# Row maxima of a forgetting-attention stage: short rows first, head 0 inside the query units

## The chip, the cores and the metric

One core of one Trainium2 chip runs the whole program; each of its engines (TensorE, VectorE, ScalarE, GpSimd, and SyncE, which issues most DMAs) has its own instruction queue. The metric is device time of one execution in microseconds; the times before are a median of three.

## The reference

A two-layer decoder trunk for one prompt of 1,040 rows (16 learned ones ahead of 1,024) and 8 decode sequences of 4 rows; width 1,024, 16 heads of 64. Layer 0 is a short gated convolution with an MLP, layer 1 forgetting attention with an MLP. Between them keys, values and the logarithms of forget values are computed. For the change only the prompt's attention counts:

```python
def forget_attention(q, k, v, c_q, c_k, q_pos, k_pos):
    s = jnp.einsum('nqhd,nkhd->nhqk', q, k) * (HEAD_DIM ** -0.5)
    s = s + (c_q.T - c_k.T)            # c = cumsum of log forget values, per head
    causal = k_pos[None, :] <= q_pos[:, None]
    s = jnp.where(causal[None, None], s, NEG_INF)
    p = jax.nn.softmax(s, axis=-1)
    return jnp.einsum('nhqk,nkhd->nqhd', p.astype(v.dtype), v)
```

## The kernel before

Every float32 matrix is split into a rounded high part (fp32r) and the difference, the low part; a product is hi*hi + hi*lo + lo*hi. A *unit* is 128 output columns of a projection: `load_unit` (SP) fetches 512 KB of weights, `round_unit` (ScalarE) makes the high part, `cut_unit` (VectorE) the low part, `unit` (TensorE) runs 72 accumulating products of 358 columns into three banks, slots alternate, and `mid` places small jobs at chosen eighths of it.

**Query units** (`U_Q` to `U_Q+7`, two heads each). Behind unit n, VectorE scales the result (`scaled`), ScalarE squares it twice (`head_squares`), VectorE takes the low part (`head_lo`), TensorE sums over each head's 64 rows (`head_sums`, at eighths 6 and 7 of the next unit, banks 6 and 7), ScalarE takes the root (`head_root`), VectorE multiplies (`head_fin`). `stage_hi` and `stage_lo` split the queries into two pairs of staging buffers, and `stage_out` writes them to DRAM (`qh_rows`, `ql_rows`), from where the heads are loaded. These pairs share their place with head 1's operands.

**Attention.** Logits are computed transposed, keys on partitions, in eight pieces per head (`GROUPS`); the softmax needs the row maximum first. So for each head `max_logits` computes the high-part logits with queries on partitions, in uses (`USES`) of one bank each, `reduce_max` (VectorE) takes their maxima, shift products (`"A"`, `"B"`, `"C"` in `USES`) turn the maxima into a row on TensorE, and `keep_shift` (ScalarE) copies that row into the query operand, negative, so that every logit comes out with the maximum taken off. The 1,040 query rows are tiled from 0 in eight tiles of 128 and one of 16. The tile of 16 rows needs three passes over all keys, 512, 512 and 16 columns. `RING = 2`: a use may start when the use two before it, in the same of banks 4 and 5, has been reduced or copied.

What sets the order is written out by hand. TensorE at turn t: logits of piece t+2, value products of piece t (`weigh_values`, three passes for each key tile), then the uses of the next head that `USE_AT[g]` names. ScalarE at turn t: two exponentials (`exp_logits`), at g = 3, 5, 7 of the piece before a `keep_shift`. VectorE at turn t: `probs_lo(t+1)`, the reductions of `USE_AT[g]`, at g = 3 the values' low part, at g = 4 `invert_sums` of the former head, at g = 7 `divide` for it.

SP per head h (`attention_loads`, L913 on): the sums of head h-1 spread to 65 partitions, its inverse stored and loaded again (`load_inverse`, L957 and L960, it waits for `invert_sums`), and only then `load_head(h + 2)` (L931 to L933, four DMAs, behind the logits of head h; the first maxima of head h+2 wait for all four, `h_loaded`), the values of a pair of heads, and `load_cross`.

```python
                if h:
                    spread_sums(h - 1)
                    load_inverse(h - 1)
                if h + 2 < HEADS:
                    load_head(h + 2)
```

Head 0 has no head before it. After the last query unit TensorE waits for three constants that ScalarE rounds there (L1657 to L1659), then runs all 18 uses of head 0 one behind the other with the last unit's head sums between them, while VectorE and ScalarE also finish and stage the last two query blocks.

## Time and profile before

| | |
|---|---|
| median of three runs | 2926.96 us (2926.76 to 2930.78) |
| the profiled execution | 2932.93 us |
| its span | 2931.1 us |
| TensorE busy | 2783.4 us (95%) |
| VectorE busy | 1186.8 us (40%) |
| ScalarE busy | 786.3 us (27%) |
| granted TensorE clock, mean | 0.979 of full |

The page is of one execution. Busy times are sums over the span; the attention of the prompt lies from 1536 to 1887 us, decode attention behind it to 2057, projections and MLPs before and after. A line of the timeline is one instruction, with the idle time of its engine before it and what ended that. A granted clock of 1.00 is 2.4 GHz, 0.50 is 1.2 GHz.

### The profile page before, as it was taken

The page shows a single profiled execution, that of the slowest core. Times are in us where ns is not written, and L with a number is a line of the kernel's source. Part 1 is how long each engine was busy: PE and PEld are TensorE (multiplying, and loading weights), DVE is VectorE, ACT ScalarE, POOL GpSimd, SP SyncE. Part 2 cuts the span into 40 slices and gives each one's busy share as a digit, 9 for nine tenths or more (in the row PEclk, how much of TensorE's full clock was granted, in tenths as well). Part 3 has the DMA queues.
Part 4 walks back from the last instruction along what each step waited for, and adds up shares of the span by engine and source line. Part 5 has one row for each costly group of instructions (what it writes and reads, how often), then busy time and mean ns, then how long its engine had stood idle before and what let it go on. Part 6 is the DMA issues. An engine that isn't in the chain of part 4 may idle for free.

```text
span 2931.1 us, 41586 instructions
## 1 busy us (share of the span) xinstructions
PE 2783.4 (95%) x17026; PEld 2701.3 (92%) x17026; DVE 1186.8 (40%) x1340; ACT 786.3 (27%) x1127; POOL 98.2 (3%) x68
## 2 busy tenths in 40 slices
PE   6999999999999999999998899767999999999999
PEld 5999999999999999998996888645999999999998
DVE  4444435224133243343346777543343133242331
ACT  4111121111011112362355566543321011110111
POOL 3000020000000001100000000000110000000000
PEclk9999999999999999999998999888999999999999
DMA  3111111111111111143244454332111111111112
GB/s 98 45 47 46 43 44 43 43 43 49 45 43 43 43 46 48 44 156 113 62 147 115 122 119 96 88 119 72 36 38 49 43 43 43 43 50 43 44 43 74
DMA packets 256005, 188.52 MB, mean 64 GB/s; under 512 B 15088, under 2 KB 237232, under 8 KB 255906
## 3 DMA queue, kind: packets, MB, share of 16 engines
q1 hardware_dynamic: 236802, 178.14, 21.5%
q10 hardware_dynamic: 19104, 8.99, 1.1%
q8 instruction: 71, 1.16, 0.2%
q14 instruction: 28, 0.23, 0.0%
HBM read 156.47 MB, written 30.49 MB: 64 GB/s over the span
## 4 chain that ended last, share of the span: by engine, by line
PE 88%; DVE 3%; DMA 3%; ACT 2%; issue 1%; POOL 1%; SPq 1%; ACTq 0%; DVEq 0%; POOLq 0%
PE ps L416 77%; DMA q_hi_ext<-k_hi_ext 2%; PE ps L878 1%; PE ps L801 1%; PE ps L579 1%; DVE max_parts L597 1%; POOL t L451 1%; PE ps L638 1%; PE ps L715 1%; PE ps L716 1%; PE ps L717 1%; PE ps L470 1%; PE ps L639 1%; DVE probs_lo L678 1%; PE ps L502 0%
## 5 line engine op out<-in xcount | busy, mean ns | idle before, releaser
L401 DVE TENSOR_TENSOR w_lo<-w_raw,w_hi 128x1024 fp32r<-128x1024 f32 x192 | 235.1, 1225 | 1233.4 <-ACT w_hi L393 1233.4
L416 PE MATMUL ps<-x_hi,w_hi 128*128 128x358 f32 x2688 | 593.8, 329 | 18.5 <-DVE x_lo L444 18.4
L416 PE MATMUL ps<-x_hi,w_lo 128*128 128x358 f32 x2688 | 590.3, 328 | 0.0
L416 PE MATMUL ps<-x_lo,w_hi 128*128 128x358 f32 x2688 | 589.5, 328 | 0.0
L393 ACT ACTIVATE w_hi<-w_raw 128x1024 fp32r<-128x1024 f32 x192 | 203.4, 1060 | 1325.2 <-PE ps L416 1324.4
L416 PEld LDWEIGHTS ps<-x_hi,w_hi 128*128 128x128 f32 x2688 | 465.4, 191 | 22.1 <-DVE x_lo L444 11.8
L416 PEld LDWEIGHTS ps<-x_lo,w_hi 128*128 128x128 f32 x2688 | 466.6, 190 | 0.0
L416 PEld LDWEIGHTS ps<-x_hi,w_lo 128*128 128x128 f32 x2688 | 465.9, 190 | 0.0
L416 PE MATMUL ps<-hid_hi,w_hi 128*128 128x358 f32 x1920 | 423.4, 329 | 3.1 <-DVE hid_lo L1234 3.1
L416 PE MATMUL ps<-hid_hi,w_lo 128*128 128x358 f32 x1920 | 420.8, 327 | 0.0
L416 PE MATMUL ps<-hid_lo,w_hi 128*128 128x358 f32 x1920 | 420.2, 327 | 0.0
L416 PEld LDWEIGHTS ps<-hid_hi,w_hi 128*128 128x128 f32 x1920 | 332.5, 190 | 3.3 <-issue 3.3
L416 PEld LDWEIGHTS ps<-hid_hi,w_lo 128*128 128x128 f32 x1920 | 332.7, 190 | 0.0
L416 PEld LDWEIGHTS ps<-hid_lo,w_hi 128*128 128x128 f32 x1920 | 332.0, 190 | 0.0
L1475 ACT ACTIVATE hid_hi<-t 128x1074 f32 (+1 forms) x72 | 79.4, 1103 | 291.1 <-DVE t L1783 260.2
L1697 DVE TENSOR_TENSOR hid_lo<-t,hid_hi 128x1074 f32 (+1 forms) x72 | 92.0, 1278 | 100.1 <-ACT hid_hi L1475 100.1
L579 PE MATMUL ps<-k_hi_ext,q_hi_ext 128*128 128x512 f32 (+5 forms) x240 | 89.5, 397 | 41.4 <-DVE max_parts L597 12.8
L451 POOL TENSOR_TENSOR t<-t,t 128x1074 f32<-128x1074 f32 x25 | 70.3, 2811 | 1275.8 <-ACT t L435 1275.4
L597 DVE TENSOR_REDUCE max_parts<-ps 128x1 f32<-128x512 f32 (+5 forms) x176 | 96.2, 563 | 39.0 <-PE ps L582 21.1
L1757 DVE TENSOR_TENSOR acc<-ps,acc 128x1074 f32 (+1 forms) x80 | 101.6, 1270 | 22.4 <-PE ps L416 22.4
L678 DVE TENSOR_TENSOR probs_lo<-probs_f,probs_hi 128x768 fp32r<-128x768 f32 (+3 forms) x128 | 97.7, 764 | 23.8 <-ACT probs_hi L666 15.6
L579 PEld LDWEIGHTS ps<-k_hi_ext,q_hi_ext 128*128 128x128 f32 (+1 forms) x240 | 41.8, 178 | 62.0 <-DVE max_parts L597 23.6
(228 smaller groups left out, 2461.9 us busy)
## 6 DMA issues: line engine op xcount, KB each, us to landing
w_raw<-in_mlp_w SPq DMA_DIRECT2D x128, 512.0 KB, 3.8
w_raw<-in_conv_w_in SPq DMA_DIRECT2D x24, 512.0 KB, 3.6
w_raw<-in_w_kv SPq DMA_DIRECT2D x16, 512.0 KB, 4.7
k_page<-in_cache_k SPq DMA_DIRECT2D x16, 512.0 KB, 4.2
v_page<-in_cache_v SPq DMA_DIRECT2D x16, 512.0 KB, 4.2
kh_rows<-staged_hi SPq DMA_DIRECT2D x8, 520.0 KB, 2.6
kl_rows<-staged_lo SPq DMA_DIRECT2D x8, 520.0 KB, 3.1
qh_rows<-staged_hi SPq DMA_DIRECT2D x8, 520.0 KB, 2.6
```

The lines of the kernel that those rows point to most:

```text
L393: act.activation(WH[:, s], RAW[:, s], ACT.Copy).then_inc(w_hi, 1)
L401: dve.tensor_tensor(WL[:, s], RAW[:, s], WH[:, s].bitcast(F32), ALU.subtract).then_inc(w_lo, 1)
L416: mm = pe.matmul(PS[:, G * s + g, 0:GW], w[:, s, k], x[:, k, g * GW:(g + 1) * GW], start=(k == 0 and n == 0), stop=(k == KC - 1 and n == 2))
L451: pool.tensor_tensor(T2[:, 0:T], T2[:, 0:T], squares(f, m), ALU.add).then_inc(x_ssq, 1)
L470: mm = pe.matmul(PS[:, b, 0:GW], weights[:, :], x[:, g * GW:(g + 1) * GW], start=not stop, stop=stop)
L579: mm = pe.matmul(PS[0:rows, bank, 0:b - a], QA[hh][:, P * i:P * i + rows], CK[hh][:, a:b], start=True, stop=not diagonal)
L597: dve.tensor_reduce(to, PS[0:rows, bank, 0:b - a], mybir.AxisListType.X, ALU.max).then_inc(red_done, 1)
L638: mm = pe.matmul(PS[0:keys, b, col:col + n], CK[hh][:, k], QA[hh][:, q0:q0 + n], start=True, stop=False)
L678: dve.tensor_tensor(PBL[:, t % HI_RING, 0:nb * w], PF[:, t % 2, 0:nb * w], PBH[:, t % HI_RING, 0:nb * w].bitcast(F32), ALU.subtract).then_ ...
L1475: act.activation(HH[:, j], T1[:, :], ACT.Copy).then_inc(hid_hi, 1)
L1697: dve.tensor_tensor(HL[:, j], T1[:, :], HH[:, j].bitcast(F32), ALU.subtract).then_inc(hid_lo, 1)
L1757: dve.tensor_tensor(banks(ACC[:, m]), result(c), banks(ACC[:, m]), ALU.add).then_inc(unit_read, 1)
```

## The change

1. **Tiling of the maxima.** Rows 0 to 15 are the short tile, tiles 1 to 8 have 128 rows from row 16 on (`max_rows`). Keys 0 to 15 of all rows go into one bank, use `"M"`: nine products of 16 columns and one of the mask, two reductions. The other uses begin at key 16. 18 uses become 16; part A now covers rows 0 to 399, B to 783, C the rest. Each part has one joining reduction (`JOIN_AT`).
2. **Place of the uses.** `weigh_values` runs a use behind each key tile's three passes, no longer all behind the last.
3. **Head 0.** Its uses go into query units 4 to 7 (`FIRST_USES`), in banks 6 and 7, their reductions and shifts into VectorE's and ScalarE's query turns; the head sums there wait for them. Behind the last unit come part C, the logits of pieces 0 and 1, then the head sums.
4. **Order of the hand-over.** ScalarE does the exponentials of pieces 0 and 1 ahead of the last root; finishing, staging and one weight split of VectorE go behind the first value pieces.
5. **Staging.** The last two query blocks use a third pair of buffers (`staged_in`), in the places of `INV` and `OS`; head 0's loads go on SP behind the fifth weight load, head 1's before the last two stagings; SP waits for both before head 2's loads.
6. **Constants.** The identity is one fp32r tile; the sign moves into `keep_shift` (scale -1); the mask takes the place of `ones` during attention and `ones` is set again behind it.

```diff
-USES = [(i, 0, P * (i + 1)) for i in range(4)]
-USES += [(i, a, b) for i in (4, 5) for a, b in ((0, 512), (512, P * (i + 1)))] + ["A"]
-USES += [(i, a, b) for i in (6, 7) for a, b in ((0, 512), (512, P * (i + 1)))]
-USES += [(8, 0, 512), "B", (8, 512, SEQ), (8, SEQ, NPR), "C"]
+USES = ["M", (1, 0, 128), (2, 0, 256), (3, 0, 384), (4, 0, 512), (5, 0, 512), (5, 512, 640), (6, 0, 512), "A",
+        (6, 512, 768), (7, 0, 512), "B", (7, 512, 896), (8, 0, 512), (8, 512, SEQ), "C"]
...
+JOIN_AT = {3: "A", 9: "B", 14: "C"}
+USE_AT = [(0, 1), (2, 3), (4, 5), (6, 7, 8), (9, 10), (11, 12), (13, 14), (15,)]
+FIRST_USES = [(), (), (), (0, 1, 2, 3), (4, 5, 6, 7), (8, 9, 10, 11), (12, 13, 14), (15,)]
...
+            elif x == "M":
+                for i in range(1, NT):
+                    q, rows = max_rows(i)
+                    pe.matmul(PS[:, bank, TAIL * (i - 1):TAIL * i], QA[hh][:, q:q + rows], CK[hh][:, 0:TAIL],
+                              start=True, stop=True)
+                to = PS[0:TAIL, bank, P:P + TAIL]
+                pe.matmul(to, QA[hh][:, 0:TAIL], CK[hh][:, 0:TAIL], start=True, stop=False)
+                mm = pe.matmul(to, IDR[:, 0:TAIL], MASK[:, 0:TAIL], start=False, stop=True)
...
-            mm.then_inc(pv_done, 1)
+                done = j == GROUPS[g][-1][1]
+                if done:
+                    mm.then_inc(pv_done, 1)
+                k = j - GROUPS[g][0][1]
+                for u in uses[k:] if done else uses[k:k + 1]:
+                    max_logits(h + 1, u)
...
+        def staged_in(n):
+
+            return 2 if n >= 2 * KC - 2 else n % 2
...
+            probs_lo(0)
             dve.wait_ge(vo_ones, 4)
             values_lo(0)
-            probs_lo(0)
             for t in range(NG * HEADS):
                 h, g = divmod(t, NG)
                 if t + 1 < NG * HEADS:
                     probs_lo(t + 1)
+                if t == 0:
+                    head_fin(2 * KC - 1, 1, G_QN, QS[:, KC - 1])
+                    stage_lo(2 * KC - 2, QS[:, KC - 2, 0:NPR])
...
+                if t == 1:
+                    cut_unit(U_O + 1)
+                    stage_lo(2 * KC - 1, QS[:, KC - 1, 0:NPR])
...
+            first_max(KC - 1)
+            pe.wait_ge(unit_read, U_O - 1)
+            logits(0)
             pe.wait_ge(unit_read, U_O)
-            for u in range(NUSE):
-                max_logits(0, u)
-                if u == 4:
-                    for f in norm_sums.values():
-                        f()
-            logits(0)
             logits(1)
+            pe.wait_ge(nm_kept, N_SH)
+            for f in norm_sums.values():
+                f()
```

TensorE's queue, head 0's first value pieces with head 1's first maxima (`probs` products are the value pieces, `k_hi_ext`/`q_hi_ext` products into `ps` the maxima). Before:

```order
L717 MATMUL ps<-probs_lo,v_hi 128x384
L715 MATMUL ps<-probs_hi,v_hi 128x256
L716 MATMUL ps<-probs_hi,v_lo 128x256
L717 MATMUL ps<-probs_lo,v_hi 128x256
L715 MATMUL ps<-probs_hi,v_hi 128x128
L716 MATMUL ps<-probs_hi,v_lo 128x128
L717 MATMUL ps<-probs_lo,v_hi 128x128
L579 MATMUL ps<-k_hi_ext_57,q_hi_ext_56 128x128
L582 MATMUL ps<-mask,ident_r 128x128
L579 MATMUL ps<-k_hi_ext_57,q_hi_ext_56 128x256
L582 MATMUL ps<-mask,ident_r 128x128
```

The same place in the changed kernel:

```order
L731 MATMUL ps<-probs_lo,v_hi 128x384
L587 MATMUL ps<-k_hi_ext_57,q_hi_ext_56 128x16 x8
L590 MATMUL ps<-k_hi_ext_57,q_hi_ext_56 16x16
L591 MATMUL ps<-mask,ident 16x16
L729 MATMUL ps<-probs_hi,v_hi 128x256
L730 MATMUL ps<-probs_hi,v_lo 128x256
L731 MATMUL ps<-probs_lo,v_hi 128x256
L596 MATMUL ps<-k_hi_ext_57,q_hi_ext_56 128x128
L599 MATMUL ps<-mask,ident 128x128
L729 MATMUL ps<-probs_hi,v_hi 128x128
L730 MATMUL ps<-probs_hi,v_lo 128x128
L731 MATMUL ps<-probs_lo,v_hi 128x128
```

The head's first maximum, which waits for the loads, moved from behind the third value tile to behind the first, and is now eight products of 16 columns with 128 rows loaded for each.

ScalarE's queue from the last query turn on (`squares`, `t_r`: the two squares; `t<-ps,eps` and `t<-t`: the root; `probs`: exponentials). Before:

```order
L1561 ACTIVATE squares_90<-k_work 128x1074 [waits z_fin,unit_read]
L1563 ACTIVATE t_r<-k_work 128x1074 [waits z_fin]
L1657 ACTIVATE mask<-mask_f_149 128x128 [waits p_const]
L1658 ACTIVATE ident_r<-ident 128x128
L1659 ACTIVATE minus_ident<-ident 128x128
L1569 ACTIVATE staged_hi_61<-q_all 128x1040 [waits st_kept0,z_fin]
L393 ACTIVATE w_hi<-w_raw 128x1024 [waits unit_done,w_loaded1]
L1575 ACTIVATE t_83<-ps,eps 128x358 [waits aux_done] x3
L1578 ACTIVATE t_83<-t_83 128x1074 [waits aux_read]
L1569 ACTIVATE staged_hi_63<-q_all 128x1040 [waits st_kept1,z_fin]
```

In the changed kernel:

```order
L1581 ACTIVATE squares_91<-k_work 128x1074 [waits z_fin,unit_read]
L1583 ACTIVATE t_r<-k_work 128x1074 [waits z_fin]
L675 ACTIVATE probs_f_115<-ps 128x768 [waits st_done]
L680 ACTIVATE probs_hi<-ps 128x768
L704 ACTIVATE v_hi<-v_raw 128x9x64 [waits v_loaded]
L675 ACTIVATE probs_f_115<-ps 128x768 [waits st_done]
L680 ACTIVATE probs_hi<-ps 128x768
L1595 ACTIVATE t_84<-ps,eps 128x358 [waits aux_done] x3
L1598 ACTIVATE t_84<-t_84 128x1074 [waits aux_read]
L1589 ACTIVATE staged_hi_123<-q_all 128x1040 [waits z_fin]
L403 ACTIVATE w_hi<-w_raw 128x1024 [waits unit_done,w_loaded1]
L1589 ACTIVATE staged_hi_123<-q_all 128x1040 [waits st_kept0,z_fin]
```

Two pairs of exponentials and the first values now stand before the root; two stagings and a weight rounding stand behind it, ahead of the exponentials of piece 2.

VectorE's queue in the changed kernel behind the last head's low part (`k_work` squares), where the maxima of head 0 stood before:

```order
L711 TENSOR_TENSOR v_lo<-v_raw,v_hi 128x9x64
L692 TENSOR_TENSOR probs_lo<-probs_f_115,probs_hi 128x768
L1859 SCALAR_TENSOR_TENSOR q_all<-k_work,vectors,t_84 128x1074
L1866 TENSOR_TENSOR staged_lo_124<-q_all,staged_hi_123 128x1040
L610 TENSOR_REDUCE max_parts<-ps 128x8
L612 TENSOR_REDUCE row_max<-ps 16x1
L617 TENSOR_REDUCE max_parts<-ps 128x1
L692 TENSOR_TENSOR probs_lo<-probs_f_115,probs_hi 128x768
L617 TENSOR_REDUCE max_parts<-ps 128x1 x2
L622 TENSOR_REDUCE row_max<-max_parts 128x3
L411 TENSOR_TENSOR w_lo<-w_raw,w_hi 128x1024
L1866 TENSOR_TENSOR staged_lo_124<-q_all,staged_hi_123 128x1040
```

Its last finishing, two stagings and a weight split stand between the first differences of probabilities.

## Rows read from the trace of the kernel before

**Rows 1.** The page, chain that ended last: shares by line.

```profile
PE ps L416 77%; DMA q_hi_ext<-k_hi_ext 2%; PE ps L878 1%; PE ps L801 1%; PE ps L579 1%; DVE max_parts L597 1%; POOL t L451 1%; PE ps L638 1%; PE ps L715 1%; PE ps L716 1%; PE ps L717 1%; PE ps L470 1%; PE ps L639 1%; DVE probs_lo L678 1%; PE ps L502 0%
```

**Rows 2.** Table by stretch: length, busy us by engine, granted clock, DMA share, GB/s.

```profile
1510.30:1523.20 12.90, 12.90 (x81) 12.90 (x79) 6.09 (x5) 6.84 (x9) 0.00 (x0) 1.00 0.55 158
...
1540.00:1550.00 10.00, 6.65 (x20) 5.15 (x20) 6.91 (x12) 4.58 (x9) 4.20 (x5) 0.50 0.47 161
```

**Rows 3.** Chain in order of time: start us, us, what; the last query unit's last stretch.

```profile
1534.70 1.50 PE ps L416 x9
```

**Rows 4.** Timeline of PE, start of attention: start us, us, instruction, [idle before].

```profile
1540.53 0.48 PE L579 MATMUL ps<-k_hi_ext,q_hi_ext 128*128 128x128 f32 x1 [4.34 <-ACT minus_ident L1659]
...
1565.33 0.41 PE L715 MATMUL ps<-probs_hi,v_hi 128*128 128x384 f32 x1
...
1573.16 0.28 PE L715 MATMUL ps<-probs_hi,v_hi 128*128 128x256 f32 x1
```

**Rows 5.** Groups by line, 1250 to 1950 us: busy us, mean ns, idle before.

```profile
L661 ACT ACTIVATE probs_f<-ps 128x768 f32<-128x768 f32 (+3 forms) x128 | 84.8, 663 | 37.8 <-PE ps L639 19.1 <-PE ps L642 18.1
...
L1575 ACT ACTIVATE t<-ps,eps 128x358 f32<-128x358 f32 x42 | 22.1, 558 | 53.4 <-PE ps L470 53.4
...
L1563 ACT ACTIVATE t_r<-k_work 128x1074 fp32r<-128x1074 f32 x13 | 14.3, 1102 | 1.7
...
L1825 DVE TENSOR_TENSOR squares_r<-squares,t_r 128x1074 fp32r<-128x1074 f32 x7 | 9.0, 1279 | 8.7 <-ACT t_r L1563 8.7
```

**Rows 6.** Timeline of PE, one head's period, 1671 to 1693 us.

```profile
1671.24 0.29 PE L715 MATMUL ps<-probs_hi,v_hi 128*128 128x256 f32 x1
...
1672.42 0.33 PE L579 MATMUL ps<-k_hi_ext,q_hi_ext 128*128 128x128 f32 x1 [0.37 <-DMA q_hi_ext<-k_hi_ext]
...
1679.70 0.40 PE L573 MATMUL ps<-minus_ident,row_max 128*1 128x128 f32 x4
...
1680.78 0.45 PE L579 MATMUL ps<-k_hi_ext,q_hi_ext 128*128 128x384 f32 x1 [0.39 <-ACT q_hi_ext L618]
...
1685.99 0.40 PE L579 MATMUL ps<-k_hi_ext,q_hi_ext 128*16 128x512 f32 x1 [0.79 <-DVE max_parts L597]
...
1692.89 0.33 PE L579 MATMUL ps<-k_hi_ext,q_hi_ext 128*128 128x128 f32 x1 [0.72 <-DMA q_hi_ext<-k_hi_ext]
```

**Rows 7.** Timeline of SP's queue in that period: the store, the last head load.

```profile
1684.77 0.36 SPq L957 DMA_DIRECT2D inv_rows<-inv_spread  x1
...
1688.38 0.56 SPq L933 DMA_DIRECT2D q_hi_ext<-k_hi_ext  x1
```

**Rows 8.** Timelines of ACT and of DVE in that period, behind part A.

```profile
1680.14 0.58 ACT L618 ACTIVATE q_hi_ext<-ps 1x512 fp32r<-1x512 f32 x1 [2.35 <-PE ps L573]
...
1682.46 0.72 DVE L678 TENSOR_TENSOR probs_lo<-probs_f,probs_hi 128x544 fp32r<-128x544 f32 x1
```

**Rows 9.** Timeline of PE: products of 16 columns, two forms.

```profile
1668.00 0.17 PE L579 MATMUL ps<-k_hi_ext,q_hi_ext 128*16 128x16 f32 x1
1668.03 0.17 PE L582 MATMUL ps<-mask,ident_r 128*16 128x16 f32 x1
...
1669.58 0.26 PE L716 MATMUL ps<-tail_hi,v_lo 128*128 128x16 f32 x1
1669.69 0.26 PE L717 MATMUL ps<-tail_lo,v_hi 128*128 128x16 f32 x1
```

**Rows 10.** Timeline of PE: first maxima of three other heads.

```profile
1607.35 0.33 PE L579 MATMUL ps<-k_hi_ext,q_hi_ext 128*128 128x128 f32 x1 [1.44 <-DMA q_hi_ext<-k_hi_ext]
...
1834.21 0.33 PE L579 MATMUL ps<-k_hi_ext,q_hi_ext 128*128 128x128 f32 x1 [1.01 <-DMA q_hi_ext<-k_hi_ext]
...
1855.54 0.33 PE L579 MATMUL ps<-k_hi_ext,q_hi_ext 128*128 128x128 f32 x1 [1.54 <-DMA q_hi_ext<-k_hi_ext]
```

**Rows 11.** Table by stretch, one us (columns as in rows 2).

```profile
1609.00:1610.00 1.00, 1.00 (x7) 1.00 (x6) 1.00 (x2) 0.00 (x0) 0.00 (x0) 0.50 0.50 74
```

**Rows 12.** Timeline of SP's queue: the store in the head of 1607.

```profile
1621.25 0.35 SPq L957 DMA_DIRECT2D inv_rows<-inv_spread  x1
```

More of the change, by code:

```diff
@@ L175, in trunk @@
         WL, _ = place("w_lo", [P, 2, KC, P], F32R)
-        ident, _ = place("ident", [P, P])
+        IDR, _ = place("ident", [P, P], F32R)
+        ident = IDR[:, :].bitcast(F32)
+        ones0 = at[0]
         ones, _ = place("ones", [P, P], F32R)
+        MASK, _ = place("mask", [P, P], F32R, offset=ones0)
         heads1, _ = place("ones_per_head", [P, P], F32R)
@@ L540, in head, with bank_of, reds_through @@
             return h // 2, h % 2
-        def use_of(h, u):
-            x = USES[u]
-            n_sh = sum(isinstance(y, str) for y in USES[:u + 1])
-            return x, 4 + u % RING, (N_RED * h + u + 1 - n_sh, N_SH * h + n_sh)
+        def bank_of(h, u):
+            return (4 if h else 6) + u % RING
+        def reds_through(h, u):
+            return N_RED * h + sum(REDS[:u + 1])
         def ring_wait(h, u):
@@ L1089, in attention_scalar @@
         def attention_scalar():
-            keep_shift(0, "A")
-            values_hi(0)
-            keep_shift(0, "B")
-            keep_shift(0, "C")
-            for t in range(NG * HEADS):
+            for t in range(2, NG * HEADS):
                 exp_logits(t)
@@ L1915, in _ @@
                 head_lo(U_Q, KC + n, n % 2)
-                if n:
+                if n == KC - 1:
+                    for hh in range(2):
+                        _, other = halves(hh)
+                        dve.memset(VH[:, hh, NT - 1, other].bitcast(F32), 0.0).then_inc(v_zero, 1)
+                    dve.memset(P8H[:, :, :].bitcast(F32), 0.0).then_inc(v_zero, 1)
+                    dve.memset(P8L[:, :, :].bitcast(F32), 0.0).then_inc(v_zero, 1)
+                    dve.wait_ge(v_zero, 5)
+                    for hh in range(2):
+                        _, other = halves(hh)
+                        dve.memset(VH[0:LASTP, hh, NT - 1, other].bitcast(F32), 1.0).then_inc(v_zero, 1)
+                elif n:
+                    for u in FIRST_USES[n][0:2]:
+                        reduce_max(0, u)
                     stage_lo(KC + n - 1, QS[:, n - 1, 0:NPR])
+                    for u in FIRST_USES[n][2:]:
+                        reduce_max(0, u)
                     cut_unit(U_Q + n + 2)
@@ L2058, in _, with first, norm @@
             unit(U_Q + 1, mid=head_sums(U_Q, 0, ax(AX_Q, 0, 0), KC))
-            with pe.Fori(1, KC // 2) as i:
-                unit(U_Q, i, mid=head_sums(U_Q, 1, ax(AX_Q - 3, 6, i), KC + 2 * i - 1))
-                unit(U_Q + 1, i, mid=head_sums(U_Q, 0, ax(AX_Q, 6, i), KC + 2 * i))
+            for n in range(1, KC - 1):
+                sums, mid = head_sums(U_Q, n % 2, ax(AX_Q + 3 * n, 0, 0), KC + n), {}
+                for k in range(len(FIRST_USES[n])):
+                    def first(n=n, k=k):
+                        first_max(n, k)
+                    mid[2 + k] = first
+                def norm(n=n, f=sums[6]):
+                    if FIRST_USES[n]:
+                        pe.wait_ge(red_done, reds_through(0, FIRST_USES[n][-1]))
+                        pe.wait_ge(nm_kept, sum(USES[u] in SHIFTS for u in range(FIRST_USES[n][-1] + 1)))
+                    f()
+                unit(U_Q + n + 1, mid={**mid, 6: norm, 7: sums[7]})
             attention_tensor(head_sums(U_Q, 1, ax(AX_Q + 3 * (KC - 1), 0, 0), 2 * KC - 1))
```

305 lines of the change are left out of this document (154 added, 151 removed).

## The prediction

> **What bounds the kernel now.** I read the page first: its chain of waits lies 77% on the projection products, and the one entry that is not arithmetic is a DMA at 2%, the last of the four loads of a head [rows 1]. The table by stage shows where TensorE is not full: during the query projection a unit of 12.9 us is full while VectorE works 6.1 us of it, so there is room for more; from 1540 us TensorE works 6.65 us of 10 at a granted clock of 0.50 [rows 2]. The chain in order of time gives the end of the last query unit, 1534.70 + 1.50 = 1536.20 us [rows 3]. The timeline of TensorE then shows the gap: the first maxima 4.34 us later, the first value product at 1565.33, that of the fourth piece of head 0 at 1573.16 [rows 4]. So two things can be won: this gap, 29.1 us for 13 maxima of head 0 and their turns on three engines; and the waits in heads 1 to 15.
>
> For a head in full swing I read the timeline of one period [rows 6] beside SP's queue [rows 7]. Its maxima begin when the loads land, at 1672.42. 12.35 us later, at 1684.77, SP can store the inverse of the former head's sums, and only behind that it issues the next head's loads; they land at 1692.89, 8.1 us after the store. The next maxima wait for them, here 0.72 us. From 1607.35 to 1855.54 [rows 10] twelve periods take 248.2 us, 20.7 each. So this is a ring of two parts: **load to store** (TensorE, ScalarE, VectorE) and **store to load** (DMA). A second ring is TensorE alone: 20.5 us in this period without the 0.72 is 19.75, in which it also idles 0.39 for ScalarE and 0.79 for VectorE [rows 6], and in shorter waits.
>
> **The change part by part.**
>
> *Head 0's maxima in units 4 to 7.* 4,608 columns; two value pieces in the timeline that are three passes of 256 and three of 128 columns take from 1671.24 to 1672.05 [rows 6], about 0.12 us per 256 columns, so 2.2 us; 8 mask products at 0.11 (0.9), 7 shift products at 0.06 (0.4). The first-16-keys bank: eight products that load 128 fresh rows each for 16 streamed columns. The tail's products have just this form and start 0.11 us apart [rows 9]: 0.9, with two small ones 0.95. Sum **+4.4 us** at full clock, on the path since TensorE is full there. VectorE's reductions, some 1.5 to 2 us a unit, are hidden by the 6.8 us it is idle in a unit [rows 2]. Head 0's eight loads are moved on SP to before three weight loads; a weight load behind them may land some 2 us later than its rounding wants it, which costs nothing while the unit before it runs. The head sums of these units now also wait for the last reduction, since both use the same two banks; it ends about 1 us before they are due.
>
> *From the last unit to the fourth piece.* Now ScalarE's and VectorE's turns decide. A full pass takes 1.10 us on ScalarE, 1.28 on VectorE, an exponential 0.66 to 0.8, a root piece 0.56 [rows 5]. From the unit's end: scaling, to 1.6; two squares, to 3.9; the low part, to 5.3; head sums on TensorE, to 6.4. ScalarE meanwhile does two pairs of exponentials and the first values, to 7.8, then the roots, to 9.5; the value products may start. Logits of piece 2 come first, at half clock after that idle: value products at 10.9 (before: 29.1). Then ScalarE has root pass, staging, a weight rounding, staging, to 13.8, exponentials of piece 2 to 15.4; VectorE follows with the difference (1.0), two reductions (1.0), a weight difference and a staging (2.5): 19.8, then 0.5 for piece 3. The fourth piece's value products start at 20.3 instead of 37.0: **-16.7 us**. The staging that went behind is the price inside this term: without it they would start near 17. SP now waits for the last staging too before it loads head 2; that is stored some 24 us after the unit's end, and head 0's last logits, for which these loads wait anyway, come no sooner.
>
> *One head's period.* Load to store: 7.3 us from the first maximum to the shift products of part A before [rows 6]. The change adds the 16-key bank (0.95) and the second and third value pieces, which now stand behind it (0.7 to 0.8), takes away 256 columns and a mask (0.2) and about 0.3 net of short waits: 8.3. From A to the store it was 5.1: the copy of the shifts starts 0.44 after A and takes 0.58, then two exponentials, and VectorE begins the next difference (0.72) at 1682.46 [rows 8], behind a values difference, then two reductions of 512. Now VectorE stands ready when ScalarE ends, and one reduction is of 256 columns: 4.4. Sum 12.7 against 12.35. Part two, 8.1 us, is untouched: the loads still stand behind the store on SP. Ring: 20.8. TensorE's own ring gets shorter: two passes of 512 and the lone 16 columns go (-0.55), the bank comes (+0.95), the waits of 0.79 and 0.39 and the shorter ones go (-1.7), some 0.3 of new ring waits come: 19.75 becomes about 18.7. So **TensorE will stand still some 2 us at each head's first maximum**, where it now stands 0.2 to 0.7 in most: the time won in the head is returned to the DMA. Behind the waiting product stand the other two value pieces and the next piece's logits, so nothing fills the wait; the exponentials, two pieces ahead, run dry too.
>
> *What that wait does to the clock.* In the present trace waits of 1.44 and 1.54 us in this place [rows 10] are each followed by half clock (0.50 at 1609 [rows 11], the lower of the two levels, 1.2 GHz), after 1.01 it stays full. The store after the 1.44 us wait came at 1621.25 [rows 12], 13.9 us after the first maximum instead of 12.35: 1.5 us lost. I take that for every head: 12.7 + 1.5 + 8.1 = 22.3 us against 20.7, times twelve, **+19 us**. Lower end of this term 0 (no drop: 20.8), upper +27 (the store-to-load part 8.8 as in the head of 1607).
>
> For the price of the eight small products a rule speaks against mine. The Trainium skill, "TensorE: Matmul & The Clock Gate", section on the back-to-back issue gap, gives matmuls of 1 to 64 columns about 60 cycles, 25 ns at the full clock; by it alone the bank would take 0.25 us and the sum would be about 9 us lower. The rows show 0.11 where 128 rows are loaded anew and 0.03 where 16 are [rows 9], so the rule alone does not hold for this form.
>
> *Rest.* Between the fourth piece and head 2's first maximum, short waits gone and the maximum placed earlier: -1.5. After the last first maximum: -0.3. Restoring the ones: +0.1.
>
> **Sum:** 4.4 - 16.7 + 19 - 1.5 - 0.3 + 0.1 = **+5**. The profiled execution took 2932.9 us (span 2931.1), 6.0 above the median of the three runs, 2926.96; the difference is applied to the median: 2932.
>
> **The rivals.**
>
> *A, forecast (55%)*: as above. Its own range is 2922 to 2940: 0.4 us either way in load to store and 0.4 in the clock's cost are some 9 us over twelve heads. Of it 8 points are faster, 27 same, 20 slower.
>
> *B, the clock holds (27%)*: the wait at the first maximum is under about 1.2 us in most heads, because load to store is 0.8 shorter than I make it or the drop needs more than idle time. For it: only three drops are seen, all beside a 0.75 us idle some 7 us earlier, which the change removes. Against it: every wait of 1.4 or more dropped, and right behind the wait now comes the bank of tiny products. Time: without the 19, 2913 to 2916. Faster.
>
> *C, the small products cost 0.03 each (6%)*: the weight loads hide. Bank 0.3 instead of 0.95, twelve times: 2924. It decides if the loads of the eight hide behind their products; the first of the four tail rows says they do once in a while. By the rule quoted above from the Trainium skill it would come out so.
>
> *D, slower (7%)*: one mechanism, SP's chain. In the head of 1607 the loads landed 8.8 us after the store, not 8.1. If the loads, now asked for by a TensorE that does nothing else, land like that in all heads, the period is 23.0 and the time 2941. It decides from 8.3 us on.
>
> *E, the change does not do what it says at the start (5%)*: the maxima are ready but piece 0 still waits on ScalarE, whose roots stand behind exponentials that wait for the values' load. Half of the 16.7 is lost: 2940.
>
> **How the numbers follow.** About 0.2%, 6 us, is what a measurement of this kernel can tell from no change. Faster 0.08 + 0.25 (B) + 0.02 (C) = 0.35; same 0.27 + 0.02 + 0.04 = 0.33; slower 0.20 + 0.07 + 0.05 = 0.32. The predicted time is A's. The range takes in B and most of D and E: 2908 to 2943.
>
> **What would show it.** First maximum's wait in each head: A 1.7 to 2.5 us and 0.50 clock behind it, B under 1.2 and full clock. Bank of eight: 0.95 us. First maximum to store: 12.7 at full clock, 14.2 with a drop. First value product 10.9 us after the last query unit, fourth piece at 20.3. Query units with maxima about 1.1 us longer each, no idle in them. If the waits of 0.79 and 0.39 are still there, the period's working is wrong; if the store-to-load part is shorter than 7.5 us, the whole term is.

## The result, and the profile after

The changed kernel takes **2952.5 us** (median of 4 runs, 2948.8 to 2958.8) beside 2928.9 us of the kernel before on the same chip: ratio 1.0083, 95% interval 1.0063 to 1.0103. It is slower by 24 us. The forecast was 2932 with a range up to 2943. The profiled execution took 2952.93 us, its span 2951.1 at a mean granted clock of 0.967; before it was 2931.1 at 0.979. The difference of the two spans, 20.0 us, is what the points below account for.

The chain that ended last, here by engine, from the page of the changed kernel, does not show where the time went; it follows another branch than in [rows 1], its shares add up to about a third of the span, and the DMA is at 0%:

```profile
PE 33%; ACT 1%; DVE 1%; issue 1%; DMA 0%; POOL 0%; ACTq 0%; DVEq 0%; POOLq 0%; SPq 0%
```

The waits of TensorE between 1595 and 1850 us do show it (waited for, us in total, times, longest); first the kernel before:

```profile
PE ps L579 <- DVE max_parts L597: 10.5, 13, 1.1
PE ps L579 <- DMA q_hi_ext<-k_hi_ext: 7.4, 11, 1.6
PE ps L579 <- ACT q_hi_ext L618: 4.6, 12, 0.4
PE ps L579 <- DVE row_max L597: 1.6, 10, 0.2
```

and the same view of the changed kernel, its one entry of any size:

```profile
PE ps L587 <- DMA q_hi_ext<-k_hi_ext: 18.8, 12, 2.5
```

TensorE now waits less in sum (18.8 us for 24.1), but in one piece per head. The granted clock in the table by stretch over the same 255 us (columns as in [rows 2]), before:

```profile
1595.00:1850.00 255.00, 229.21 (x1636) 210.45 (x1636) 194.36 (x360) 153.14 (x311) 0.00 (x0) 0.99 0.49 112
```

and now:

```profile
1595.00:1850.00 255.00, 236.16 (x1548) 221.71 (x1546) 168.31 (x325) 140.33 (x281) 0.00 (x0) 0.87 0.47 107
```

So TensorE is busier (236 us for 229) and gets less done (1548 entries for 1636): behind its waits it runs at the lower level. Counted by single microseconds, half clock (0.50, 1.2 GHz) fills 10 us between 1595 and 1870 before, 68 us now, in all twelve heads, eight times for 6.8 us and four times for 3.4. One head's period in the timeline of TensorE, against [rows 6, 10]:

```profile
1668.42 1.06 PE L587 MATMUL ps<-k_hi_ext,q_hi_ext 128*128 128x16 f32 x8 [1.35 <-DMA q_hi_ext<-k_hi_ext]
1669.33 0.17 PE L590 MATMUL ps<-k_hi_ext,q_hi_ext 128*16 128x16 f32 x1
...
1679.65 0.37 PE L582 MATMUL ps<-ident,row_max 128*1 128x16 f32 x4
...
1691.67 1.06 PE L587 MATMUL ps<-k_hi_ext,q_hi_ext 128*128 128x16 f32 x8 [1.57 <-DMA q_hi_ext<-k_hi_ext]
```

and SP's queue in it, against [rows 7]: the store of the inverse, and the last of the four loads that the first maximum waits for.

```profile
1683.84 0.35 SPq L987 DMA_DIRECT2D inv_rows<-inv_spread  x1
...
1687.94 0.56 SPq L963 DMA_DIRECT2D q_hi_ext<-k_hi_ext  x1
```

First maximum to part A 11.2 us (before 7.3), to the store 15.4 (12.35), store to the next first maximum 7.8 (8.1): a period of 23.25 here. Over twelve heads the mean is (1872.32 - 1598.40) / 12 = 22.8 us; before it was 20.7.

The start, from the timeline of TensorE, against [rows 3, 4]: the end of the last query unit, the first value product, that of the fourth piece.

```profile
1540.38 0.65 PE L426 MATMUL ps<-x_hi,w_lo 128*128 128x358 f32 x3
...
1553.85 0.63 PE L729 MATMUL ps<-probs_hi,v_hi 128*128 128x384 f32 x1
...
1566.24 0.39 PE L729 MATMUL ps<-probs_hi,v_hi 128*128 128x256 f32 x1
```

### The profile page after: what moved, and what is told of

Same layout as the page of the kernel before. It is cut to its first block and busy times, and to the rows that moved or that the text cites. A ratio compares the mean times of both kernels' runs of the same rounds, so it can differ in the third digit from the quotient of the medians.

```text
span 2951.1 us, 41757 instructions
## 1 busy us (share of the span) xinstructions
PE 2815.4 (95%) x17122; PEld 2741.9 (93%) x17122; DVE 1175.4 (40%) x1342; ACT 786.5 (27%) x1125; POOL 99.3 (3%) x68
## 5 line engine op out<-in xcount | busy, mean ns | idle before, releaser
L426 PEld LDWEIGHTS ps<-x_hi,w_hi 128*128 128x128 f32 x2688 | 464.6, 190 | 22.4 <-DVE x_lo L454 11.8
L617 DVE TENSOR_REDUCE max_parts<-ps 128x1 f32<-128x512 f32 (+1 forms) x192 | 105.8, 554 | 63.6 <-PE ps L599 54.6
L729 PE MATMUL ps<-probs_hi,v_hi 128*128 128x272 f32 (+4 forms) x272 | 100.9, 371 | 1.7 <-DVE probs_lo L692 1.5
L652 PE MATMUL ps<-q_hi_ext,k_hi_ext 128*128 128x272 f32 (+5 forms) x288 | 97.9, 345 | 0.8 <-ACT t L1595 0.7
```

Of the source, the lines that this page charges most:

```text
L426: mm = pe.matmul(PS[:, G * s + g, 0:GW], w[:, s, k], x[:, k, g * GW:(g + 1) * GW], start=(k == 0 and n == 0), stop=(k == KC - 1 and n == 2))
L617: dve.tensor_reduce(NMX[:, i - 1, k:k + 1], PS[:, bank, 0:b - a], axis, ALU.max).then_inc(red_done, 1)
L652: mm = pe.matmul(PS[0:keys, b, col:col + n], CK[hh][:, k], QA[hh][:, q0:q0 + n], start=True, stop=False)
L729: pe.matmul(to, VH[:, hh, j], ph, start=(j == 0), stop=False)
```

## The experiments

All times are medians, the ratios are to the kernel before on the same chip; its own median lay between 2928.9 and 2934.1 us in the different series, so a distance of two medians from different series carries up to 5 us of that, which the ratios do not. "Period" is the mean distance of the first maxima of neighbouring heads in the profiled execution. "Half clock" is counted by single microseconds, over the stretch named.

**1. The loads of the next head but one ahead of the inverse sums (in SP's queue), in the changed kernel.**

```
     if h: spread_sums(h - 1)
-    if h: load_inverse(h - 1)
     if h + 2 < HEADS: load_head(h + 2)
+    if h: load_inverse(h - 1)
```

> The changed kernel with one step moved in SP's queue: the loads of head h+2's keys and queries are issued before the load of the inverse sums of head h-1, behind which they stand now (they then wait only for the logits of head h that read the same buffers). Ring theory: the 1.1 to 2.5 us wait at each head's first maximum is the store-to-load ring (7.8 us from the store to the landing); with the loads ahead of it the wait is under 0.3 us in most heads, the clock stays at its upper level, the period falls from 22.8 to 18.7 to 20 us, and the time to 2905 to 2920. Rival 'the placement itself is slow' (the uses between the value pieces, or the small products, stretch the head): the wait goes but the period stays over 22 us, time within 8 us of the changed kernel. Rival 'the transfers are bound by the DMA': the loads land no earlier, the wait stays.

2927.6 us, ratio 0.9990 (0.9977 to 1.0002): 25 us under the changed kernel. The profiled execution took 2917.8 us, the fastest of ten (up to 2935.8). In it no wait for the loads is left and the period is 20.3 us. The theory holds for the ring, but the period and the median are above the expected ranges, since a new wait came, for VectorE's difference (TensorE's waits in this run):

```profile
PE ps L729 <- DVE probs_lo L692: 17.8, 13, 2.2
```

The waits of VectorE name what holds that difference back: the division stands ahead of it in VectorE's order, and the inverse sums, whose load now lies behind the head's loads, come late.

```profile
DVE q_all L760 <- DMA inv_sums<-inv_rows: 40.7, 13, 4.0
```

**2. Products that fill the wait.** Seven 128x512 products whose results nothing reads, ahead of the wait for the loads. They write into the bank of the first maxima, so the wait for that bank, `ring_wait(h, u)`, which stood last, moves ahead of them; the kernel computes nothing else differently.

```
+    ring_wait(h, u)
     if u == 0:
+        if h > 2:
+            for _ in range(7): pe.matmul(PS[:, bank, 0:512], VH[:, 1 - hh, 0], CK[1 - hh][:, 0:512], ...)
         pe.wait_ge(h_loaded[hh], 64 * (h // 2 + 1))
-    ring_wait(h, u)
```

> The changed kernel with seven products of 128x512 more in every head from the fourth on, whose results nothing reads, placed before the wait for the loads at the first maximum; they take about 1.5 us of TensorE at full clock. The wait itself is untouched, so this tells the clock's part from the wait's. If the idle at the first maximum is what drops the granted clock, the 7 us of half clock behind it go, load to store falls from about 15.3 to about 12.7 us, and the period from 22.8 to about 20.8: time 2925 to 2935 although TensorE does more. If the drop comes from something else (the bank of eight products with 16 columns, or the thin work of the whole head), the half clock stays and the time is that of the changed kernel or up to 10 us more.

2924.9 us, ratio 0.9973 (0.9962 to 0.9983). TensorE does some 1.5 us more in each of 13 heads and the kernel is 28 us faster than the changed one. The loads land no sooner after the store (8.2 us in the mean for 8.0), but the clock holds in nine of the twelve heads from 1595 us on:

```profile
1595.00:1850.00 255.00, 250.68 (x1768) 231.31 (x1767) 182.06 (x354) 150.87 (x305) 0.00 (x0) 0.97 0.50 114
```

In the heads without a drop first maximum to part A is 8.1 us and to the store of the inverse 12.0 to 12.3 (in one 8.5 and 12.7); the period is 20.0 to 20.3 in six of the nine, and up to 21.9 in the other three, whose next loads land later. That is the changed kernel's ring at full clock, and it is shorter than the 20.7 us of the kernel before. The loss against that kernel is therefore the clock's.

**3. The maxima behind the value piece again**, everything else as changed.

```
-                k = j - GROUPS[g][0][1]
-                for u in uses[k:] if done else uses[k:k + 1]:
-                    max_logits(h + 1, u)
+            for u in uses:
+                max_logits(h + 1, u)
```

> The changed kernel, but every head's maxima of a turn stand behind the whole value piece again, not between its parts, as in the kernel before; order of the maxima, first-keys bank and head 0 stay changed. If the wait at the first maximum rules, the maxima come 0.7 to 0.8 us later into the head and the loads wait is the same or shorter: time within 5 us of the changed kernel. If placing them between the value pieces is itself the loss, the time falls by 10 us or more. If it was a gain hidden in the sum, it rises by about 5 to 10 us, the short waits of 0.4 and 0.8 us for ScalarE and VectorE coming back.

2935.1 us, ratio 1.0016 (1.0002 to 1.0030): 17 us faster than the changed kernel, which the theory did not expect. The value products now stand ahead of the waiting product and fill part of the wait, so waits are 0.65 to 1.45 us in most heads where they were 1.1 to 1.6:

```profile
PE ps L587 <- DMA q_hi_ext<-k_hi_ext: 14.6, 12, 2.5
PE ps L582 <- DVE max_parts L617: 3.4, 12, 0.3
```

Half clock between 1595 and 1870 falls from 68 to 44 us, and first maximum to part A at full clock is 7.75 instead of 8.1. 24 us less half clock are 12 us of time, twelve times 0.35 are 4: most of the 17. The forecast had named that nothing fills the wait behind the first maximum and priced that at nothing.

**4. The same move of the loads in the kernel before.**

> The kernel before with the same one step moved in SP's queue as in the first of these runs. Ring theory: here the ring is nearly balanced by TensorE's own 19.75 us, so moving the loads takes away waits of 0.2 to 0.7 us in most heads, 1.4 in two, and the three drops of the clock: period from 20.7 to about 19.8, time 2914 to 2920. Against the changed kernel with the same step this gives what the change is worth without the ring: by the theory the changed one is then 5 to 12 us faster. If the rival holds that the change itself stretches the head, the changed kernel with this step stays slower than this one.

2965.6 us, ratio 1.0115 (1.0098 to 1.0132): 34 us slower than the kernel before, a miss. Its period is 23.2 us:

```profile
PE ps L579 <- DVE row_max L597: 27.7, 11, 3.0
PE ps L579 <- DVE max_parts L597: 8.5, 11, 0.8
```

The theory took the landing of the loads for the only thing on SP's queue that matters. VectorE waits 2.6 us in the mean for the inverse sums in the division; the differences and the reductions of the row maxima stand behind it.

**5, 6. Both moves: loads ahead, and the division one turn later on VectorE**, in the changed kernel and in the kernel before.

```
-    if h and g == 7:
-        divide(h - 1)
+    if h > 1 and g == 0:
+        divide(h - 2)
```

> The changed kernel with the loads of head h+2 ahead of the inverse sums in SP's queue, and now also the division of head h-1, which waits for those sums, one turn later on VectorE, behind the next difference instead of ahead of it. With the loads alone moved, the division waited 3.2 us and held back the difference behind it, and TensorE stood 1.1 to 1.7 us for that difference in every head. Ring theory: this wait goes too, waits of TensorE over 0.5 us vanish from most heads, half clock between 1595 and 1870 us falls from 20 us to under 7, the period from 20.2 to 18.8 to 19.3 us, time 2905 to 2915. Rival 'VectorE itself is full there': the difference comes late again behind the division, one turn further, the period stays over 20 us and the time within 5 us of the run with the loads alone moved (2928).

> The kernel before with both moves (loads ahead of the inverse sums, division one turn later). If the division's wait is what made the loads-first version of the kernel before 34 us slower (period 23.2 us, TensorE 2.2 to 3.0 us idle for the first row maxima), that wait goes, and the period falls to TensorE's own ring of about 19.8 us: 2915 to 2922. The changed kernel with both moves should then be 5 to 12 us faster than this one, which is what the change is worth when no DMA stands in its ring. If the change has another loss in it, this one is the faster of the two.

Changed kernel: 2903.1 us, ratio 0.9891 (0.9874 to 0.9907). Kernel before: 2924.1, ratio 0.9963 (0.9951 to 0.9976). Each is 2 us outside its expected range (2905 to 2915, 2915 to 2922), the first below and the second above, so the change is then worth 21 us, more than the 5 to 12 expected. The undisturbed period is 18.1 us (for instance 1671.52 to 1689.66 between two first maxima) against 20.0 to 20.1 in the kernel before with both moves. Half clock in the changed kernel's heads is 14 us, not under 7: two heads wait 2.2 us for ScalarE, and a drop of 6.8 us follows in each. TensorE's waits in the changed kernel with both moves, and in the kernel before with them:

```profile
PE ps L652 <- ACT probs_hi L680: 5.6, 3, 2.2
PE ps L582 <- DVE max_parts L617: 0.9, 3, 0.3
```

```profile
PE ps L579 <- DVE max_parts L597: 10.4, 13, 1.1
PE ps L579 <- DVE row_max L597: 5.5, 12, 0.5
PE ps L579 <- ACT q_hi_ext L618: 5.0, 13, 0.4
```

So the change does in the head what it says: the waits for ScalarE and VectorE go. In the kernel as it was, the ring through SP's queue took all of it.

**7. The division later, alone**, the fourth corner of the square.

> The changed kernel with the division one turn later alone; the loads stay behind the inverse sums in SP's queue. This is the fourth corner of the square of the two moves (neither 2953, loads alone 2928, both 2903). Theory: the ring through SP still stands, so TensorE still waits 1.1 to 2.5 us at each head's first maximum and the clock halves behind it: time within 5 us of the changed kernel, period 22.5 to 23. Rival 'VectorE's queue was the cause': 10 us faster or more.

2957.3 us, ratio 1.0088 (1.0064 to 1.0112), half clock 68 us between 1595 and 1870, as in the changed kernel; the waits are as they were, 20.6 us in 12. VectorE's order alone was not the cause. The four corners: neither 2952, loads 2928, division 2957, both 2903.

**8, 9. What the bank of small products costs.** Both kernels are number 5 with a second bank of eight 16-column products, whose results are written over or the same: once right behind the first, once some 3 us later, ahead of the maxima of the fourth tile.

```
-                for i in range(1, NT):
+                for i in 2 * list(range(1, NT)):
```

```
                 i, a, b = x
+                if x == (3, 0, 384):
+                    for k in range(1, NT): ...  # the eight products again, into this bank
```

> The changed kernel with both moves, where TensorE is the bound, and the eight products of 16 columns of the first-keys bank done twice in every head (same operands, same place). This measures their price. By the rows (eight take 0.95 to 1.06 us from first to next product): period 18.1 plus 0.9 to 1.0, time 12 to 15 us above that run's 2903. By the rival of hidden weight loads (0.03 us each): 3 to 4 us above it.

> The changed kernel with both moves and a second bank of eight 16-column products (results overwritten by the next product, nothing reads them), but placed before the maxima of the fourth tile's 384 keys, some 3 us behind the first bank, not in one stretch with it. Work is the same as in the run with the bank twice (period 19.0 us at full clock). If thin products in one stretch of 1.9 us act on the clock like an idle of that length, the seven drops seen there go to two or fewer: half clock between 1595 and 1850 us under 10 us, time 2908 to 2914. If it is their number in a head, half clock stays at 20 us or more and the time at 2916.

Together: 2916.4 us (ratio 0.9940, 0.9924 to 0.9957), 13 us above number 5. The period at full clock is 19.03 for 18.13: **0.9 us for eight, 0.11 each**, as taken from [rows 9]. The Trainium skill, "TensorE: Matmul & The Clock Gate", section on the back-to-back issue gap, gives about 25 ns for products this narrow as the gap of a product taken by itself, and says that in a stream the load of the weights counts too. Where each loads 128 fresh rows, the runs say 0.11 us, which fits the second and not the first; rival C is out.

What neither theory expected is the clock. With the banks together it halves in seven of thirteen heads, and only one of these drops has an idle time of TensorE over 0.5 us ahead of it. One of the others, TensorE's timeline and then the table by stretch:

```profile
1657.94 1.85 PE L587 MATMUL ps<-k_hi_ext,q_hi_ext 128*128 128x16 f32 x16
...
1661.40 0.63 PE L729 MATMUL ps<-probs_hi,v_hi 128*128 128x384 f32 x1
```

```profile
1660.00:1661.00 1.00, 1.00 (x12) 1.00 (x10) 0.69 (x4) 0.00 (x0) 0.00 (x0) 1.00 1.28 313
1661.00:1664.00 3.00, 3.00 (x14) 3.00 (x14) 2.42 (x3) 1.82 (x4) 0.00 (x0) 0.54 1.05 230
```

With the same products apart: 2909.0 us (ratio 0.9915, 0.9899 to 0.9932), as expected; half clock between 1595 and 1850 us is 3.4 us instead of 24, its one drop behind an idle time of 2.5 us:

```profile
1595.00:1850.00 255.00, 250.57 (x1897) 236.77 (x1896) 192.84 (x378) 160.96 (x325) 0.00 (x0) 0.99 0.50 116
```

So in six of thirteen heads a stretch of 1.85 us of 16-column products, which counts as busy, was followed by a drop as idle time is, and the same products in two stretches by none.

**10, 11. Is it the wait's length, or what stands behind the wait?** In the changed kernel, the bank as the fourth of the maxima; and three filling products in place of seven.

```
-USES = ["M", (1, 0, 128), (2, 0, 256), (3, 0, 384), (4, 0, 512), ...
+USES = [(1, 0, 128), (2, 0, 256), (3, 0, 384), "M", (4, 0, 512), ...
```

> The changed kernel with the bank of eight 16-column products as the fourth of a head's maxima instead of the first; behind the wait for the loads now come products of 128 to 384 columns, as in the kernel before. The wait itself stays (1.1 to 2.5 us). If the small products behind the wait are why the half clock lasts 6.8 us in two heads of three, where it lasted 3.4 behind waits of the same length in the kernel before, it falls to 3.4 in most heads: 50 us or less of half clock between 1595 and 1870 us instead of 68, time 10 to 15 us under the changed kernel. If only the wait's length and the rest of the head decide, half clock stays over 60 us and the time within 5 us of the changed kernel.

> As the run with seven filling products before the wait, but three of them (about 0.65 us at full clock, results unused, from the fourth head on). They leave some 0.5 to 1.0 us of the wait. In the runs so far waits up to 0.85 us were followed by no half clock, 0.9 to 1.3 us by 3.4 us of it or none, 1.35 us and more by 3.4 or 6.8. Theory: the clock's cost goes by the wait's length, so half clock falls from 68 to 15 to 35 us and the time to 2930 to 2940. Rival: any wait at this place halves the clock, half clock stays over 55 us and the time over 2945.

Bank fourth: 2944.9 us (2934.2 to 2950.2; ratio 1.0037, 1.0022 to 1.0052), 8 us under the changed kernel by the medians and 13 by the ratios, at the lower end of the 10 to 15 expected or under it. Its waits are as long as in the changed kernel:

```profile
PE ps L596 <- DMA q_hi_ext<-k_hi_ext: 19.7, 12, 2.6
```

but in the profiled execution (2938.1 us, on the fast side of its ten) the clock stayed up five times behind the ten waits of 1.27 to 1.77 us, where in the changed kernel each of the twelve, from 1.08 us on, was followed by a drop. Behind the two of 2.4 and 2.6 us, and one of 1.77, half clock lasted 10 us and more. So the bank's place explains part of the double length, and a long wait is enough by itself. Three filling products: 2935.0 us (ratio 1.0004, 0.9988 to 1.0020), half clock 34 us between 1595 and 1870: five of the eight waits up to 0.83 us and the one of 0.95 were without a drop, the three of 1.25 us and more were not. Its expectation had read the runs before it too sharply: in number 2 a wait of 0.76 us was followed by a drop, and in the changed kernel one of 1.08 us by a drop of 6.8. Both parts count, and no single length decides.

**12. The last staging later, alone; 13. the same on top of number 5.**

```
+                if t == 3:
+                    stage_hi(2 * KC - 1, QS[:, KC - 1, 0:NPR])   # ScalarE, was ahead of t = 2
```

> The changed kernel with the last staging on ScalarE behind the exponentials of the third and fourth piece of head 0, nothing else. Theory: the 3.4 us wait for the one staging pair goes from the path of the start: first value product of the fourth piece near 1563 to 1564 instead of 1566.2, time 2 to 5 us under the changed kernel, the heads as they are. Rival: SP's chain (head 2's loads wait for the last staging too) gives it back, and the first maximum of head 2 comes no earlier.

> The changed kernel with both moves, and the last staging on ScalarE behind the exponentials of the third and fourth piece of head 0, where it stood ahead of them and waited 3.4 us for the store of the one staging pair it shares. Theory: at the start the fourth piece's first value product comes about 3 us earlier than 1566.2 (near 1563); the heads are untouched: 3 us off the run with both moves. Rival: VectorE's turn with the staging, which now comes later, holds back the difference of the next piece as long; the fourth piece stays near 1566 and the time is the same.

Alone: 2954.6 us (ratio 1.0075, 1.0056 to 1.0094), no gain. From the last query unit's end to the fourth piece it is 24.2 us instead of 25.2, but 0.8 of that lies ahead of the first value product, before the place where the edit acts; from there to the fourth piece it is 12.1 for 12.4, and VectorE is now the one waited for (0.93 us), so the rival was nearer. On top of number 5: 2898.1 (0.9881, 0.9865 to 0.9898), 5 us faster by the medians, with ranges that overlap (2897.3 to 2902.4 and 2899.6 to 2903.7). From the first value product to the fourth piece it is 12.4 us for 12.3, so nothing was won there; half clock between 1595 and 1850 falls from 14 to 3 us, which is worth the 5. Why those drops go, the runs do not tell.

**14, 15, 16. The best version.** Number 5 with the maxima behind the value piece; with the staging move too; and with both and the rounding of the values one turn later.

```
-                if g == 2 and h < HEADS - 1:  values_hi(h + 1)     # ScalarE
+                if g == 3 and h < HEADS - 1:  values_hi(h + 1)
-                    if g == 3:  values_lo(h + 1)                   # VectorE
+                    if g == 4:  values_lo(h + 1)
```

> The changed kernel with both moves, but each turn's maxima behind the whole value piece. In the changed kernel as it is this placement won 17 us, by the ring theory because the value products then fill part of the wait for the loads and the clock drops in fewer heads. Without the ring that reason is gone: theory expects a period 0 to 0.8 us longer than with maxima between the value parts (the short waits for VectorE come back), time 0 to 10 us above that run. If the placement between the parts is bad in itself, this one is faster again by 10 us or more.

> The same without the later rounding of the values: the staging move and the placement behind the value piece together, each of which gave 5 us alone. If they act on different stretches (start, heads) they add: 2892 to 2895. If both only take away the same wait in the first heads: 2897 to 2899, as either alone.

> The best version so far with one more move: loads ahead of the inverse sums, division a turn later, last staging later, maxima behind the value piece, and the rounding of the next head's values (ScalarE, and VectorE's half of it) one turn later. In the runs with both moves ScalarE waited 2.5 to 3.2 us for the values' load in two or three heads, TensorE stood 1.5 to 2.4 us behind it and the clock halved. Theory: these waits go, every head between 1595 and 1850 us takes 18.2 to 18.8 us: 2890 to 2895. Rival: the rounding and the copy of the shifts then meet on ScalarE and part A's copy comes late in every head: waits of 0.3 to 0.8 us for ScalarE in each, 2900 to 2905.

2898.0 us (0.9875, 0.9858 to 0.9891), 2898.1 (0.9886, 0.9870 to 0.9903), **2892.0 (0.9862, 0.9845 to 0.9878)**. Placing the maxima between the value pieces is worth nothing even without the ring: behind them it is 5 us faster, against expectation. The staging adds nothing to that. The last version, as expected for it, beats the kernel before by 1.4% and the changed one by 2%; no wait over 0.7 us is left in its heads and the clock holds:

```profile
1595.00:1850.00 255.00, 244.43 (x1853) 231.87 (x1851) 194.16 (x386) 166.30 (x341) 0.00 (x0) 1.00 0.49 116
```

## Why the prediction was wrong

The mechanism of case A was right: the ring through SP's queue holds each head's first maximum, and the clock falls behind that wait. The time fell outside the range because three terms were mis-sized, the clock's cost in the heads, the start and the end. Term by term, forecast and trace:

- **Head 0's maxima in the units, +4.4.** The last query unit ends 4.8 us later, at 1541.03; 0.3 of it lies in the execution already at 1431 us, so 4.5. Right, and no idle stood in the units.
- **Start, -16.7.** The fourth piece follows the unit's end by 25.2 us, not 20.3: -11.8. The first value product came at 12.8 instead of 10.9, which is the wait of ScalarE for the values' load (1.9 us). The other 3.0 lie between it and the fourth piece: 12.4 us where the forecast's turns of ScalarE and VectorE make 9.4. TensorE itself is busy there almost without a break, at half clock up to 1564.3, while the forecast had taken half clock for the logits of one piece alone. The table by stretch of the changed kernel, from the first value product on:

```profile
1553.85:1564.30 10.45, 10.45 (x46) 10.45 (x45) 5.59 (x10) 6.23 (x11) 0.00 (x0) 0.50 0.38 154
```

In numbers 7 and 12 half clock ended some 2 us sooner behind the first value product, and TensorE then waits 0.9 us for VectorE: 12.3 and 12.1 us. In number 16, where it ended 8 us sooner, the distance is 9.35, but other moves are in it. So VectorE stands close behind, and how the 3.0 divide is not shown. The last staging did wait 3.4 us, because the last two stagings share one pair of buffers, and the forecast had costed it on ScalarE and VectorE only, not at the store it waits for; but with that staging moved (numbers 12 and 13) the distance shrinks by 0.3 us at most. The two waits of ScalarE in the changed kernel, 1541 to 1570 us:

```profile
ACT staged_hi L1589 <- DMA ql_rows<-staged_lo: 3.4, 1, 3.4
ACT v_hi L704 <- DMA v_raw<-out_v_prompt: 1.9, 1, 1.9
```

- **From there to head 2's first maximum, -1.5.** -2.0, to the maximum from which the twelve periods are counted. It is head 3's (1607.35 before, 1598.40 now); the forecast miscounted it by one.
- **Period of twelve heads, +19.** +25.7 (22.8 for 20.7 us each, forecast 22.3). Load to store at full clock was forecast 12.7 and is 12.0 to 12.3 (numbers 2, 10 and 11); store to load 8.1 and is 8.0 in the mean, 7.8 in the head shown; the bank 0.95 and is 0.9 to 1.0; the waits of 0.39 and 0.79 are gone as said. **The step that failed is "What that wait does to the clock": the drop was priced at 1.5 us from the two long waits of [rows 10, 12].** In the changed kernel it costs 1.6 us in four heads of twelve and 3.1 in eight (first maximum to part A 9.7 or 11.2 instead of 8.1), 2.6 in the mean: 12.2 + 2.6 + 8.0 is the 22.8. Only its size was off: the waits were even shorter than forecast, 1.1 to 1.6 us in ten of twelve heads for 1.7 to 2.5, and the clock fell behind each. Numbers 8 to 10 show part of why the old rows were too cheap: behind the wait now stands the bank, almost a microsecond of products that, in a longer stretch, were followed by a drop without any wait. The forecast had put exactly this as a reason against case B ("right behind the wait now comes the bank of tiny products") and then taken the price without it. It is not all: in number 3 the bank stands behind the wait too, and waits of 1.03 and 1.27 us passed without a drop; in number 10, with the bank three maxima further on, three drops lasted 10 us and more. What sets the length of a single drop stays open.
- **After the last first maximum, -0.3.** +5.0. The last head waits longest, 3.45 us for its loads, and the half clock around that wait lasts 10 us:

```profile
1872.32 1.88 PE L587 MATMUL ps<-k_hi_ext,q_hi_ext 128*128 128x16 f32 x8 [3.45 <-DMA q_hi_ext<-k_hi_ext]
...
1897.85 0.41 PE L729 MATMUL ps<-probs_hi,v_hi 128*128 128x384 f32 x1 [1.48 <-DVE probs_lo L692]
```

The sum of the parts, 0.3 + 4.5 - 11.8 - 2.0 + 25.7 + 5.0, is 21.7; what follows the prompt's attention is 1.7 shorter, which leaves the 20.0 of the spans. The forecast's terms make 5: of the 15 missing, 6.7 are the period's, 4.9 the start's and 5.3 the end's; the other terms give 2 back. Two slips of its working changed little: the gap before held 15 maxima of head 0, not 13, and its terms for first maximum to part A make 8.5, not 8.3, where 8.0 to 8.1 was measured.

Of the rivals, B (the clock holds) did not come; number 2 gives its ring, 20.0 to 20.3 us a head, and the 2913 to 2916 named for it would have been about right: the changed kernel less half of its 68 us of half clock in the heads is 2918, an estimate. D's price, a store-to-load part of 8.8 us, was seen in three heads only (8.7 to 9.7), but its time was the nearest of all, for the wrong reason. The range was too narrow because case A's own range took 0.4 us a head for the clock's cost, when the only rows for it came from another surrounding: the upper bound should have been a drop of double length, which gives 19 + 12 x 1.6 = 38.

## What to carry to other kernels

Time won between two waits of a ring comes back as one longer wait at its slowest link; before shortening the work, find what the link waits for, here a queue on which loads that nothing held back stood behind a store. Move both ends of it: with the loads moved alone the kernel before lost 34 us, since a consumer of the displaced load blocked its own engine's order. And look where idle time and thin products gather: here, in one piece per head, they halved the clock in every head, while the waits of up to 1.14 us that the kernel before spreads over a head cost only themselves.

## What the runs showed of the hardware

TensorE's granted clock went to its lower level (0.50, 1.2 GHz) without idle time: behind 1.85 us of 16-column products in one stretch in six of thirteen heads (number 8), behind the same products in two stretches 3 us apart in none (number 9). Waits of TensorE up to 0.85 us were mostly without effect (in numbers 2 and 11 four of them, 0.65 to 0.83 us, were followed by a drop); waits of 1.0 to 1.8 us were followed by a drop in some heads and not in others, in five of ten with products of 128 to 384 columns behind them (number 10) and in all ten of the changed kernel with the bank behind them; of the thirteen waits of 2.1 to 3.0 us in number 4, ten were. Eight 16-column products that each load 128 fresh rows take 0.9 us (numbers 8 and 9). Filling a wait with 128x512 products that nothing reads made the kernel 28 us faster (number 2).
